# A compression block spread among the memory attention's steps, and position products moved to another buffer

## The reference, cut to what matters

```python
z = h @ w_in                                              # layer 0, input projection
y, h_last = s5_ssm(z[..., :SSM_WIDTH], h0, ...)           # scan over the states
om = mem_attention(z[..., SSM_WIDTH:]..., mem_kv)         # 4 heads, prompt and 8 sequences

# layer 1's compressed keys and values of the past; they depend on the cache alone
proj = cmp_subblock_proj(past_cmp, w1)                    # 'bnjhce,ajcef->bnhacf'
bias = jnp.einsum('jce,jcef->cf', pe, w1) + b1            # position products, summed
hid = proj[:, :-1, :, 0] + proj[:, 1:, :, 1] + bias
ckv = jnp.einsum('bnhcf,cfe->bnhce', jax.nn.gelu(hid), w2)
```

## Time and profile before

| | us |
|---|---|
| median of 3 runs | 1201.52 |
| lowest and highest of the 3 | 1195.62, 1202.44 |
| the profiled execution, its own time | 1197.44 |
| its span in the profile | 1195.8 |
| granted TensorE clock, mean over the span | 0.958 of full |

### The profile page before, as it was taken

The page is one execution under the profiler, slowest core; times in us unless marked ns, Lnnn a source line. Parts: engine busy times, 40 slices in busy tenths (PEclk is TensorE's granted clock), DMA queues, the critical chain, the costliest instruction groups (busy, mean ns, idle before and its releaser), DMA issues.

```text
span 1195.8 us, 16402 instructions
## 1 busy us (share of the span) xinstructions
PE 1109.1 (93%) x6032; PEld 810.3 (68%) x6032; DVE 366.4 (31%) x789; ACT 202.5 (17%) x497; POOL 242.1 (20%) x314
## 2 busy tenths in 40 slices
PE   6979999999989999999999996884888999999996
PEld 5746666666767777777767774443766777777774
DVE  5728677430142111100032104777213211110002
ACT  3310000012231000000031103554103100000000
POOL 0608567620001111130000031414400110110000
PEclk9979999999999999999999996897879999999998
DMA  8565434330425656674433344575723244333341
GB/s 321 211 211 172 144 120 121 106 107 8 175 71 186 238 217 245 263 252 153 156 141 106 109 147 125 156 267 146 211 86 122 106 141 140 130 127 113 130 145 64
DMA packets 59112, 185.13 MB, mean 155 GB/s; under 512 B 8609, under 2 KB 39586, under 8 KB 48418
## 3 DMA queue, kind: packets, MB, share of 16 engines
q1 hardware_dynamic: 52322, 165.28, 40.2%
q0 software_dynamic: 6144, 12.59, 3.6%
q10 hardware_dynamic: 576, 6.29, 1.4%
HBM read 180.35 MB, written 10.02 MB: 159 GB/s over the span
## 4 chain that ended last, share of the span: by engine, by line
PE 87%; DVE 4%; issue 2%; SPq 2%; DMA 2%; ACT 1%; POOLq 0%; POOL 0%; DVEq 0%
PE banks L718 29%; PE banks L496 16%; PE banks L758 14%; PE banks L694 14%; PE banks L516 3%; SPq L397 1%; PE banks L664 1%; PE banks L1039 1%; PE banks L849 1%; PE banks L677 1%; PE banks L562 1%; PE banks L1060 1%; SPq L393 1%; DMA phase<-in_slcv 1%; PE banks L471 1%
## 5 line engine op out<-in xcount | busy, mean ns | idle before, releaser
L718 PE MATMUL banks<-normed,slabs 128*128 128x288 f32 x1408 | 346.6, 410 | 9.1 <-ACT normed L1140 9.1
L718 PEld LDWEIGHTS banks<-normed,slabs 128*128 128x128 f32 x1408 | 270.1, 192 | 85.2 <-issue 10.0
L758 PE MATMUL banks<-hidden,slabs 128*128 128x288 f32 x704 | 171.2, 406 | 1.4 <-issue 1.4
L694 PE MATMUL banks<-arena,phase 128*128 128x384 f32 x512 | 171.7, 494 | 0.0
L758 PEld LDWEIGHTS banks<-hidden,slabs 128*128 128x128 f32 x704 | 133.6, 190 | 39.0 <-issue 2.3
L694 PEld LDWEIGHTS banks<-arena,phase 128*128 128x128 f32 x512 | 96.9, 192 | 65.4 <-issue 1.8
L1425 POOL TENSOR_TENSOR projected<-projected,rstd 128x288 f32<-128x288 f32 x44 | 34.9, 792 | 449.3 <-ACT projected L1207 449.3
L496 PE MATMUL banks<-normed,slabs 128*128 128x288 f32 (+1 forms) x416 | 106.6, 410 | 1.2 <-ACT normed L1140 1.2
L496 PEld LDWEIGHTS banks<-normed,slabs 128*128 128x128 f32 (+1 forms) x416 | 75.7, 187 | 27.1 <-issue 3.7
L1509 DVE TENSOR_TENSOR normed<-normed 128x288 f32<-128x288 f32 x24 | 11.0, 459 | 199.0 <-ACT normed L1200 199.0
L1207 ACT ACTIVATE projected<-projected 128x288 f32<-128x288 f32 x44 | 19.5, 443 | 281.4 <-DVE projected L1556 281.4
(11 more groups left out here) (293 smaller groups left out, 1071.7 us busy)
## 6 DMA issues: line engine op xcount, KB each, us to landing
slabs<-in_wfi SPq DMA_DIRECT2D x44, 1024.0 KB, 4.9
slabs<-in_w SPq DMA_DIRECT2D x25, 1024.0 KB, 4.8
arena<-in_cmp SPq DMA_DIRECT2D x128, 192.0 KB, 2.7
slabs<-in_wfo SPq DMA_DIRECT2D x32, 704.0 KB, 4.1
arena<-in_slck SPq DMA_DIRECT2D x64, 96.0 KB, 2.7
arena<-in_slck POOLq DMA_DIRECT2D x64, 96.0 KB, 2.5
out_win_old<-in_winold SPq DMA_DIRECT2D x8, 762.0 KB, 6.3
arena<-in_wink SPq DMA_DIRECT2D x4, 768.0 KB, 6.5
```

What stands on the lines that cost most here:

```text
L694: ins = nc.tensor.matmul(out.rearrange("p h (g s) -> p h g s", s=8), W1S[:, c, a, j, :], PG[b % 2][:, :, c * 8 + j, :, :].rearrange("p g h ...
L718: return nc.tensor.matmul(BK[2 * (u % SLOTS) + c][:, 0:T], wt[:, k, c * P:c * P + P], Hn[:, k, :], start=(k == 0), stop=(k == KC - 1), ski ...
L758: ins = nc.tensor.matmul(BK[b][:, 0:T], wt[:, k, :], HD[:, 11 * kh + k, :], start=(kh + k == 0), stop=(kh * 11 + k == 21))
```

## The change

The first compression block, `compress(0, 0)`, leaves the S5 stage. Its 16 matmuls are issued between the steps 7, 8 and 9 of the memory attention and `cmp_bias()`, by a function `between(i)` that is called ahead of matmul i. The loop over blocks runs from 1. What stood behind block `blk` now stands behind block `blk + 1`, except that the outputs of the last unit stand half-way through the last block. The inputs of unit 1 stand half-way through block 1.

The position products get another home: 12 x 128 columns at the start of `mixed` (M_), where the transposed memory lay for the key and value projection. Since this is smaller, GpSimd multiplies four positions at a time and adds them up as it goes, each instruction waiting for the one before. SP no longer waits for `pe_summed` ahead of sequence 0's pages.

```diff
-        PEP = AR[:, 2048:6144].rearrange("p (c q f) -> p c q f", c=2, q=16)
+        PEP = M_[:, 0:1536].rearrange("p (n f) -> p n f", f=P)
...
             s5_blocks()
-            mem_step(0, 6, 7)
-            cmp_bias()
-            mem_step(0, 6, 8)
+
+            def beside_first(i):
+                if i == 6:
+                    mem_step(0, 6, 7)
+                elif i == 7:
+                    cmp_bias()
+                elif i == 9:
+                    mem_step(0, 6, 8)
+                elif i == 13:
+                    mem_step(0, 6, 9)
+
+            compress(0, 0, between=beside_first)
...
-            mem_step(0, 6, 9)
...
             s5_in(0)
-            for blk in range(2 * B):
+
+            def beside_block(blk, i):
+                if i == 8 and blk == 1:
+                    s5_in(1)
+                elif i == 8 and blk == 2 * B - 1:
+                    s5_y(N_UNIT - 1)
+
+            for blk in range(1, 2 * B):
                 b, c = blk // 2, blk % 2
-                compress(b, c, halfway=lambda: s5_in(1) if blk == 0 else None)
+                compress(b, c, between=lambda i: beside_block(blk, i))
...
-                for n in outputs_beside(blk):
-                    s5_y(n)
-                if blk + 2 < N_UNIT:
-                    s5_in(blk + 2)
+                for n in outputs_beside(blk - 1):
+                    if n < N_UNIT - 1:
+                        s5_y(n)
+                if blk + 1 < N_UNIT:
+                    s5_in(blk + 1)
...
-            for q in range(0, 32, 4):
-                ch.tick(tt(PEP.rearrange("p c q f -> p (c q) f")[:, q:q + 4, :], U[:, P * q:P * q + 512].rearrange("p (q f) -> p q f", f=P),
-                           pr("pe")[:, q:q + 4].unsqueeze(2).to_broadcast([P, 4, P]), ALU.mult))
-            ch.sync()
...
+            for c in range(2):
+
+                for n, to in ((0, 0), (4, 4), (8, 8), (12, 8)):
+                    q = 16 * c + n
+                    ch.step(tt(PEP[:, to:to + 4, :], U[:, P * q:P * q + 512].rearrange("p (q f) -> p q f", f=P),
+                               pr("pe")[:, q:q + 4].unsqueeze(2).to_broadcast([P, 4, P]), ALU.mult))
+                    if n >= 8:
+                        ch.step(tt(PEP[:, n - 8:n - 4, :], PEP[:, n - 8:n - 4, :], PEP[:, 8:12, :], ALU.add))
+                for n in (4, 2):
+                    ch.step(tt(PEP[:, 0:n, :], PEP[:, 0:n, :], PEP[:, n:2 * n, :], ALU.add))
...
-            sp.wait_ge(pe_summed, 1)
             load_pages(0)
```

More of the change, by code:

```diff
@@ L680, in s5_y, with compress @@
                 ins.then_inc(y_full, 1)
-            def compress(b, c, halfway):
+            def compress(b, c, between):
                 key = ("hc", b, c)
@@ L689, in compress @@
                 for a in range(2):
-                    if a:
-                        halfway()
                     for j in range(8):
+                        if a + j:
+                            between(8 * a + j)
                         out = BK[5 + c][:, 0:387].rearrange("p (h n) -> p h n", n=129)[:, :, 1 - a:129 - a]
@@ L1431, in _ @@
             pool.wait_ge(prm_loaded, 16)
-            for q in range(0, 32, 4):
-                ch.tick(tt(PEP.rearrange("p c q f -> p (c q) f")[:, q:q + 4, :], U[:, P * q:P * q + 512].rearrange("p (q f) -> p q f", f=P),
-                           pr("pe")[:, q:q + 4].unsqueeze(2).to_broadcast([P, 4, P]), ALU.mult))
-            ch.sync()
[L1436 to L1442, removed]
+            for c in range(2):
[7 more added lines that the diff above has]
+                    ch.step(tt(PEP[:, 0:n, :], PEP[:, 0:n, :], PEP[:, n:2 * n, :], ALU.add))
+                ins = tt(PER[:, P * c:P * c + P], PEP[:, 0, :], PEP[:, 1, :], ALU.add)
+                if c == 0:
+                    ch.step(ins)
+                else:
+                    ins.then_inc(pe_summed, 1)
             def states(n):
```

## The result

| | before | after |
|---|---|---|
| median, us | 1198.94 (4 runs) | 1188.01 (4 runs) |
| lowest to highest | 1195.62 to 1202.44 | 1186.36 to 1188.51 |
| the profiled execution, its own time | 1197.44 | 1188.51 |
| its span | 1195.8 | 1186.9 |
| mean granted clock over the span | 0.958 | 0.959 |

The ratio after to before is 0.9908, 95% interval 0.9887 to 0.9930: 10.9 us less by the medians, 0.9%.

What follows compares the result with a forecast made beforehand. PE was taken to bound the kernel, busy 93% of the span. A gain of 11.4 us less 0.2 for late pages made 11.2, giving 1186.2 or 1190.3 by footing; 1188.5 was forecast, range 1182 to 1198.

Steps and rivals of the forecast that it cites:

- two footings: Starting times for the gain: the profiled execution, 1197.44 giving 1186.2, and the median of runs shown, 1201.52 giving 1190.3.
- the neighbour at 0.38: The whole kernel's outcome class: faster by over 1%, given chance 0.38.
- The sum: PE's new order from 70.90 at full clock: 28.66 us of work, `compress(1, 0)` at 99.56, gain 11.4 us.
- The covers: Steps 7 to 9: block 0's matmuls fill PE's waits for probabilities, values and ScalarE's copies; step 8 ends at 79.93.
- that rival: Memory attention stretch: clock still at half from 75.2 to 88.9, gain only 4.6 us, about 1195; chance 0.13.
- What is late next: At `compress(1, 0)`: sequence 1's pages, in at 98.6 to 100.5, wanted at 99.56; stall 0 to 0.9, 0.2 taken.
- The rival (late by 3.4 us): At `compress(1, 0)`: sequence 1's pages stall PE 3.4 us, leaving 8.0 of gain, about 1191.7; chance 0.13.
- The units' chain: S5 stage's end set by the units, whose first inputs come 1.4 us later; about 1201, slower; chance 0.04.
- The early pages: Input projection's last slab delayed by sequence 0's pages; over 21.9 us would eat all gain; chance 0.04.
- The queues: SP's page loop starts at 35.2 and ends near 51; early pages and the slab share DMA engines at no cost.
- The tail: End of S5: last unit's outputs come half a block nearer its inputs, 5.3 us, and the new place costs nothing.
- Its end moves by the same amount: Rest of the S5 stage keeps its block order, so its end moves by the 11.4 us gained at `compress(1, 0)`.

Runs made afterwards that it cites:

- block 0 in one piece: Changed kernel with all 16 matmuls of block 0 together ahead of step 7 instead of spread; ratio to the kernel before 0.9963.
- early pages alone: Kernel before, PE's order kept, with position products in the other buffer and sequence 0's pages requested without waiting for them; ratio to before 0.9985.
- kernel with filled gaps: Kernel before with 15 idle matmuls in PE's gaps around steps 7, 8 and 9, no work moved; ratio to before 0.9973.
- kernel with these pages late: Changed kernel with sequence 1's pages requested when step 9 of the memory attention is made instead of step 8; median 1191.13 us, ratio to before 0.9943.
- sequence 0's pages late: Changed kernel with the wait for the position products put back ahead of sequence 0's pages; ratio to the kernel before 1.0003.

## Why the prediction was right, point by point

**Forecast and range.** 1188.5 was forecast and 1188.01 measured, in a range of 1182 to 1198. The gain was put at 11.2 us against the profiled execution's time and lies at 10.9 by the medians, 8.9 by the two profiled executions. That the forecast was met to half a microsecond is in part luck: it stood half-way between two footings 4.1 apart, and the median of the kernel before came out at 1198.94, between them. I gave 0.57 to less than 1%; it is 0.9%, so near the line that the neighbour at 0.38 was as good a guess.

**The sum.** Predicted for the work from the transposes to `compress(1, 0)`: 28.66 us. Measured: 28.23 from 71.37 (the end of the transposes) to 99.60, and in it a stall of 0.07. The absolute 99.56 agreed with 99.60 only because the stretch also began 0.47 us later. That is not the pages' doing: SP's last slab request already stood 0.7 later (35.50 for 34.81), ahead of the first page. Terms that I sized too large: the bias, 0.34 in the chain for 0.64, since its old distance to step 8 held a wait; step 8, 1.88 for 2.16; the transposes, 0.22 and 0.44 for 0.30 and 0.59: 0.8 us in all. Terms too small: the blocks in pieces, 10.64 and 10.72 in the chain for 10.52 each, and with the 0.07 that is 0.4 the other way. So half of the error cancelled.

**The covers.** Step 8 was to end at 79.93 and ended at 79.73; no wait stood where I had said none. Unit 0's inputs ended at 85.93 for 86.17. That block 0 in one piece brings back 0.7 and 1.2 us shows that it is the spreading which covers ScalarE's copies.

**The clock.** Predicted at 1.00 throughout, and it was. But my argument against that rival was half wrong. I wrote that the clock fell "only in the 3.12 of idleness that the matmuls would now fill"; with early pages alone that idle time was 1.29, the clock fell just the same, and it had fallen before that gap began, behind nothing longer than 1.78 us of idleness. Behind 10 us of dense matmuls, on the other hand, gaps of 0.7 and 1.2 us left it alone (block 0 in one piece). So filling the 3.12 alone may not have kept the clock up; the change fills the 1.78 as well. Which part of the thin work and idleness ahead of 74.3 brings the clock down, no run here separates.

The Trainium skill (TensorE: Matmul & The Clock Gate, "What's actually happening") says that activity releases the throttle. The kernel with filled gaps agrees: matmuls whose results nobody reads kept 1.00 and brought 3.9 us in the trace.

**What is late next.** Sequence 1's pages were named, with a stall of 0 to 0.9 and 0.2 taken. It was 0.07; the slack is nothing, as the kernel with these pages late showed. Two things that I had otherwise cancelled: the last page took 4.3 us to land, the slow end of my 2.3 to 4.2, but SP's loop was 0.9 us shorter (13.99 for 14.90), so that the last request stood at 95.2 and not at 96.25. With the old loop the stall would have been about 1 us, an estimate from 96.25 + 4.3 - 99.53. The rival (late by 3.4 us) did not come about.

**The other rivals.** The units' chain did not set the end: VectorE still waited 58.3 us for outputs from 99 to 290, and PE waited for VectorE once between 71 and 262, 0.7 us, as in the kernel before. The early pages did not delay the input projection.

**The queues.** The page loop began at 37.89, not at 35: SP spends some 2 us between its last slab and the first page, as it did behind the two other waits, and I had left that out. The products ended at 60.46 for 59. They began 1.7 us later (38.87 for 37.20), which I had not foreseen: GpSimd stood idle 1.78 us ahead of them with no releaser in the profile. In the other seven profiled kernels with early pages that gap is 1.75 to 2.15 in four and 0.63 to 0.85 in three, in the kernel before it is 0.80, and with sequence 0's pages late there is none (start at 36.33). Why stays open. Their own length grew by 1.6, near the 2 that I took. The last slab landed 11.6 us after its request for 10.9 and was in time, and the values landed in 4.8 for 6.81: both moved the way that the prediction took from the sharing of the DMA engines. All of these had slack, so none reached the sum.

**The tail.** I costed the new place of the last outputs at nothing. It is worth 0.5 us net, since the old one would now have stood right behind another unit's outputs.

**"Its end moves by the same amount."** To the end of the stage this held: the last block ended 11.1 us sooner (277.44 for 288.54, the start of `compress_k(7)`), 11.6 by the start of the stretch. Behind it the profiled pair drifts: from there to the end of the span 907.3 us before, 909.5 after. Two rows of the changed kernel show a part:

```profile
698.72 11.70 PE L865 MATMUL banks<-projected,phase 64*128 64x45 f32 x128
...
714.80 2.85 PE L908 MATMUL banks<-cst,projected 64*128 64x15 f32 x48
```

In the kernel before these were 9.59 and 5.31 us: the clock fell in this part of layer 1 in both, only at another place in the program. The mixer's first 64 rows took 17.27 before and 18.34 after. The nine profiled executions without fillers in the mixer or behind compute the same from there on. These rows took 17.27 to 18.72 in them, and the whole way from `compress_k(7)` to the end of the span 907.3 (before), 907.8, 907.9, 908.4, 908.9 (the changed kernel's repetition), 909.5 (the changed kernel), 910.4, 910.9 and 911.1 us (block 0 in one piece). So the 2.2 us lie within what single executions differ by, and so does the 1.6 that block 0 in one piece lost besides. But the kernel before has the shortest of the nine, and the mean clock says something alike: 13.7 us at half clock taken out of the stretch would by themselves raise the mean over the span by 0.006 (an estimate, 13.7 x 0.5 / 1187), and it went from 0.958 to 0.959. The medians (10.9 for 11.8 in the stretch) leave about 1 us for such a loss. Whether the change causes it, by where it puts the later stages against the clock, stays open.

## What to carry to other kernels

A gap on the bounding engine costs twice: its own length, and the slower work around it if the clock falls. Here it was nearly 8 and about 4 us. Fill it with work that is due later, in pieces small enough to stand between the dependent steps, and check what transfer the displaced buffer or the earlier step releases, since that becomes the next wait. Where there is no work to move, idle matmuls into an unused bank give back the second part: 15 of them were worth 3 to 4 us here, and two sets of nine ahead of the mixers about as much by the medians, with intervals that overlap.

## What the runs showed of the hardware that I had not expected

- With early pages alone the granted clock fell at 74.3, behind idle gaps of 0.47 and 1.78 us with short work between and after them, and ahead of the next gap; it did not fall with 0.7 and 1.2 us behind 10 us of dense matmuls.
- The same 64 rows at the first mixer's entry took 17.3 to 18.7 us in nine executions, and 15.76 in both mixers of both kernels when the gap ahead of them was filled.
- Pages requested at addresses read from a table cost SP about 0.9 us each: 14.0 to 16.0 us for 16. From the end of step 8 to the first of them there were another 1.8 us, and that loop, more than bandwidth, set when sequence 1's pages were in: the transfers moved 195 GB/s in 86 to 88, where the earlier trace rows has 365 in 26 to 40.
